# Summing a matrix-vector product over the partitions: products in column strips of the array in place of one-column products

## The chip, the cores and the metric

One core of a Trainium2 chip. The metric is the device time of one execution of the whole kernel in microseconds, the median of several runs; less is better.

## The reference, cut to what matters

A block of DEPTH = 2 layers with adaptive normalisation is followed by a second block that has none. All is fp32, D = 1024, 512 tokens. The part of the change is the first line of each layer of the first block:

```python
cond = jax.nn.silu(c)                                   # (1, 1024)
for i in range(DEPTH):
    mod = (cond @ ada_w[i] + ada_b[i]).reshape(b_, 3, 3, D_MODEL)   # ada_w[i]: (1024, 9216)
    h = adaln(x, norm_g[i, 0], mod[:, 0, 0], mod[:, 0, 1])
    x = x + 0.5 * (1.0 + mod[:, 0, 2][:, None, :]) * swiglu(h, ffn_w_in[i, 0], ffn_w_out[i, 0])
    ...
```

So `mod` holds 9 vectors of 1024 for each layer, 18 in all: shift, scale and gate of three sublayers.

## The kernel before, in words

The activations lie transposed in SBUF, 1024 channels as 8 chunks (DC) of 128 partitions, 512 tokens along the free dimension. Each large product is done in split precision: ScalarE (ACT) rounds a unit of weights (8 x 128 x 128, loaded by SyncE (SP) into one of four stages) to `w_hi` (L778), VectorE (DVE) subtracts to `w_lo` (L1325), and TensorE (PE) does three fp32r products for each chunk (L2060 to L2062; L2075 to L2077 for the first two units behind a norm), 24 matmuls of 512 columns a unit. A step of a feed-forward's first half (`step_in`) is four units, and there are eleven steps (`FC // 2`). `w_hi` and `w_lo` have two sides, so ACT converts a unit when the unit two before it is done.

The conditioning product is not done on PE as a matrix product. `cond` lies as one column for each of the 8 chunks of channels; DVE multiplies a piece of 128 rows and 512 columns of `ada_w` by its scalars and adds it to `ada_acc` (128 x 1024), 16 instructions a vector (`ada_add`, L1338 and L1341). Then `ada_acc` holds, for each of the vector's 1024 elements, 128 parts, one for each partition, and they must be summed over the partitions so that element c * 128 + q lands in partition q, column c. That is `ada_sum` on PE (L2081 to L2088): eight fp32 products, each with a 128 x 128 piece of `ada_acc` as the stationary operand and one column of ones as the moving one, into eight columns of bank 7 (`MODS`). `ada_finish` on DVE (L1344 to L1350) waits for it and adds the bias into `mod`.

The first two vectors (shift and scale of the first norm, `ADA_FIRST = 2`) are made ahead of everything, in `ada_first_acc` (128 x 2048): eight DVE instructions (L2014 to L2022), then `first_modulation` on PE (L2673 to L2679), 16 products behind the statistics of the first norm, while DVE waits at L2025 and adds the bias at L2026. The first norm needs its result: gain (L1358), `sg` (L1391), `h_hi`, `h_lo`, the first products.

The other 16 vectors are made one a step: 7 in the first seven steps of the first feed-forward and 9 in the first nine steps of the second (`ADA_IN = {0: 7, 1: 9}`), all well ahead of their use. The order of work in a step is written out by hand for each engine. DVE does for each of the four units: the conversion of the unit two ahead, for odd ones the product of gate and up (L1443), its share of the 16 additions (`ADA_ADDS = [6, 10, 16, 16, 16]`, the first 6 ahead of the first conversion), `a_lo` (L1450); `ada_finish` comes last in the step. PE does its four units and then `ada_sum`. SP issues the pieces of `ada_w` between the loads of weights, into a ring of eight slots, each freed by the addition that read it (L611); its first load waits for the first modulation (L613). `pe.wait_ge` in `ada_sum` asks that all 16 additions are done and that the vector before was finished; the first addition of a vector waits for the sum of the one before (L1337).

Other places that are compared with: attention's weighing (`weigh`), plain fp32 products with a stationary operand of 64 columns. In L2242 the products of a head follow one another into the same 64 partitions of a bank; in L2604 two heads alternate, one into partitions 0 to 63 and one into 64 to 127, each with widths of 512, 384, 128 and 256. An fp32 product takes two matmul instructions, an fp32r one takes one. DVE at shapes like those of the change: L1548 reduces 128 x 512 from PSUM to one column, L1724 multiplies 128 x 256.

Of the kernel before, what the change touches and what calls it, by code (L numbers as in the profile page):

```python
# [23 lines left out]
ALU = mybir.AluOpType  # L24
ACT = mybir.ActivationFunctionType
AX = mybir.AxisListType

P = 128
S = 512
D = 1024  # L30
DC = D // P
# [10 lines left out]
ADA_FIRST = 2  # L42
# [5 lines left out]
def vec_columns():  # L48

    col, at = {}, 0  # L50
    for name, n in [("c", 8), ("ada_b", 144), ("norm_g", 48), ("pool_scale", 8), ("ln_mix", 16), ("ln_ffn", 16),
# [7 lines left out]

VEC, NVEC = vec_columns()  # L60
CONST = {"ident": 0, "ones": P, "blk64": 2 * P, "blk32": 3 * P, "rot32": 4 * P, "rot96": 5 * P, "mask": 6 * P,
         "dft": 7 * P}
NCONST = 9 * P


class Tally:
# [27 lines left out]
def build(nc, A, out):  # L94
    ctx = ExitStack()
    with ctx:
        def sem(name):
            return ctx.enter_context(nc.semaphore(name))
# [40 lines left out]
        ada_acc = at("ada_acc", [P, D], F32, "ada", 4 * ADA_COLS * 4)  # L139
        ada_first_acc = at("ada_first_acc", [P, ADA_FIRST * D], F32, "ada")  # L140
# [7 lines left out]
        def small(name, n, dt=F32):  # L148
            t = at(name, [P, n], dt, "small", small_at[0])
            small_at[0] += (n * {BF16: 2, U8: 1}.get(dt, 4) + 31) // 32 * 32  # L150
            assert off["small"] + small_at[0] <= SLAB, name
            return t

        vec = small("vec", NVEC)
        consts = small("consts", NCONST)
        ident, ones, blk64, blk32, rot32, rot96, mask = (
            consts[:, CONST[c]:CONST[c] + P] for c in ("ident", "ones", "blk64", "blk32", "rot32", "rot96", "mask"))
        dft = consts[:, CONST["dft"]:CONST["dft"] + 2 * P]
        negident_r = small("negident_r", 16, F32R)
        ident_bf = small("ident_bf", P, BF16)  # L160
        mask_bf = small("mask_bf", P, BF16)
# [8 lines left out]
        mod = small("mod", 18 * DC)  # L170
# [3 lines left out]
        zero = small("zero", DC)  # L174
        eps = small("eps", 1)
        gs = small("gs", S)

        bank = [ctx.enter_context(nc.psum_tensor(f"bank{i}", [P, S], F32)) for i in range(8)]
        GATE, UP, Y, MODS = bank[0:2], bank[2:4], bank[4:6], bank[7]
# [32 lines left out]
        ada_first_added = sem("ada_first_added")  # L212
        mod_summed = sem("mod_summed")
        mod_ready = sem("mod_ready")
        dve_chain = sem("dve_chain")
        x_in_t = sem("x_in_t")
        out_t = sem("out_t")
# [1090 lines left out]
        def _(dve):  # L1308
            n = Tally()
# [18 lines left out]
            def ada_add(m, v=0):  # L1328
# [10 lines left out]
                else:  # L1339
                    dve.wait_ge(ada_added, v * ADA_PER_VEC + u - 1)  # L1340
                    nc.vector.scalar_tensor_tensor(acc, w, cond[:, k:k + 1], acc, ALU.mult, ALU.add) \  # L1341
                        .then_inc(ada_added, 1)

            def ada_finish(v=0):  # L1344
                dve.wait_ge(mod_summed, n.vec - ADA_FIRST + v + 2)
                col = (n.vec + v) * DC
                dst = mod[:, col:col + DC] if isinstance(v, int) else mod[:, bass.ds(col, DC)]
                b = vec[:, VEC["ada_b"] + col:VEC["ada_b"] + col + DC] if isinstance(v, int) else \
                    vec[:, bass.ds(col + VEC["ada_b"], DC)]
                nc.vector.tensor_tensor(dst, MODS[:, 0:DC], b, ALU.add).then_inc(mod_ready, 1)  # L1350

            def norm(s):

# [660 lines left out]
            for k in range(DC):  # L2014
                dve.wait_ge(ada_first_loaded[k], 16)
                if k == 0:
                    ins = nc.vector.tensor_scalar(ada_first_acc[:], ada_first[:, k], cond[:, k:k + 1], None, ALU.mult)
                else:
# [4 lines left out]
            convert(0)  # L2023
            convert(1)
            dve.wait_ge(mod_summed, 1)  # L2025
            nc.vector.tensor_tensor(mod[:, 0:ADA_FIRST * DC], MODS[:, 0:ADA_FIRST * DC],  # L2026
                                    vec[:, VEC["ada_b"]:VEC["ada_b"] + ADA_FIRST * DC], ALU.add) \
                .then_inc(mod_ready, ADA_FIRST)
            n.vec = ADA_FIRST
# [19 lines left out]
        def _(pe):  # L2049
            n = Tally()  # L2050
# [15 lines left out]
            def first_pair(dsts, cols=(P, P)):  # L2066
# [3 lines left out]
                for k in range(DC):  # L2070
                    pe.wait_ge(h_ready, (n.norm - 1) * DC + k + 1)
                    for a, dst in enumerate(dsts):
# [5 lines left out]
                        if k == DC - 1:  # L2078
                            ins.then_inc(unit_done, 1)

            def ada_sum(v=0):  # L2081

                pe.wait_ge(ada_added, (n.vec - ADA_FIRST + v + 1) * ADA_PER_VEC)
                pe.wait_ge(mod_ready, n.vec + v)
                for c in range(DC):
                    ins = nc.tensor.matmul(MODS[:, c:c + 1], ada_acc[:, c * P:(c + 1) * P], ones[:, 0:1],  # L2086
                                           start=True, stop=True)
                ins.then_inc(mod_summed, 1)  # L2088

            def busy_work(spare, count):  # L2090

# [581 lines left out]
            def first_modulation():  # L2673

                pe.wait_ge(ada_first_added, DC)
                for c in range(ADA_FIRST * DC):
                    ins = nc.tensor.matmul(MODS[:, c:c + 1], ada_first_acc[:, c * P:(c + 1) * P], ones[:, 0:1],
                                           start=True, stop=True)
                ins.then_inc(mod_summed, 1)  # L2679

            n.vec = ADA_FIRST
            for step in STAGE_ORDER:
# [14 lines left out]
            for t in range(TB):  # L2697
                for g in range(2):
                    if 2 * t + g >= 4:
                        pe.wait_ge(out_copied, 2 * t + g - 3)  # L2700
                    for d in range(4):
                        c = 4 * g + d
# [67 lines left out]
def constants():  # L2770

    c = np.zeros((P, NCONST), np.float32)
    i = np.arange(P)

    def put(name, a):
        c[:a.shape[0], CONST[name]:CONST[name] + a.shape[1]] = a
    put("ident", np.eye(P))
    put("ones", np.ones((P, P)))
    put("blk64", i[:, None] // 64 == i[None] // 64)
    put("blk32", i[:, None] // 32 == i[None] // 32)  # L2780

    first = (i % 32) < 16
    rot = -1.0 * ((i[:, None] == i[None] + 16) & first[None]) + ((i[:, None] == i[None] - 16) & ~first[None])
    put("rot32", rot)
    rot96 = rot.copy()
    rot96[:64] = rot96[:, :64] = rot96[96:] = rot96[:, 96:] = 0
    put("rot96", rot96)
    put("mask", np.where(i[:, None] >= i[None], 0.0, -1e30))

    f = 2 * np.pi * (i[:, None] * i[None] % 64) / 64  # L2790
    scale = (i[:, None] // 64 == i[None] // 64) / np.sqrt(64.0 * S)
    put("dft", np.concatenate([np.cos(f) * scale, np.sin(f) * scale], 1))
    t = np.arange(S)
    g = 2 * np.pi * (t[:, None] * t[None] % S) / S
    seq = np.stack([np.cos(g), -np.sin(g)]).astype(np.float32)
    bands = []
    for w in (2, 4, 8, 16):
        reach = (i[None] - i[:, None] >= 0) & (i[None] - i[:, None] < w)
        bands += [reach / w - np.eye(P), reach / np.minimum(i + 1, w)[None] - np.eye(P),
                  ((P + i[None] - i[:, None] < w) / w)[:, 0:16]]  # L2800

    inv = (1.0 / (np.float32(10000.0) ** (np.arange(0, 32, 2, dtype=np.float32) / np.float32(32)))).astype(np.float32)
    ang = inv[:, None] * t.astype(np.float32)[None]
    cos, sin = np.tile(np.cos(ang), (2, 1)), np.tile(np.sin(ang), (2, 1))
    rope_m = np.stack([np.concatenate([np.ones((64, S)), cos]), np.concatenate([np.zeros((64, S)), sin])])
    rope_d = np.stack([np.tile(cos, (4, 1)), np.tile(sin, (4, 1))])

    masks = [(i[:, None] // (2 * h) == i[None] // (2 * h)) & (i[:, None] // h != i[None] // h)
             for h in (64, 32, 16, 8, 4, 2, 1)] + [i[:, None] == i[None]]
    return {"consts": c, "dft_seq": seq, "pool_band": np.concatenate(bands, 1).astype(np.float32), "rope_m": rope_m.astype(np.float32),  # L2810
            "rope_d": rope_d.astype(np.float32), "hgrn_mask": np.concatenate(masks, 1).astype(np.float32)}
# [21 lines left out]
```

## Time and profile before

| what | value |
|---|---|
| median of 3 runs | 3809.81 us (3807.85 to 3809.84) |
| span of the profiled execution, first to last instruction | 3808.2 us |
| time of that execution by itself | not among the three listed |
| busy: PE, PE loads of weights, DVE, ACT, POOL | 98%, 77%, 46%, 36%, 3% |
| mean granted TensorE clock | 0.990 |
| DMA | 390 MB, mean 103 GB/s |

Times in the profile are counted from the first instruction. Engines are named PE (TensorE's matmuls), PEld (its loads of weights, which overlap them), DVE, ACT, POOL (GpSimd) and SP. L with a number is a line of the kernel. A matmul's duration in the profile is modelled and longer than the distance to the next one, so the price of a run of matmuls is read from starts.

### The profile page before, as it was taken

Reading aid. Unit: us, or ns where it says so; the run is one execution under the profiler, and the core shown is the slowest. Engines: PE = TensorE matmul, PEld = TensorE weight load, DVE = VectorE, ACT = ScalarE, POOL = GpSimd, SP = SyncE. Lnnn points to the kernel's source line nnn. Section 1 sums busy time; section 2 is a strip of 40 time slices with the busy share of each in tenths; the row PEclk is TensorE's granted clock in tenths of the full one; section 3 lists DMA queues with packets and bytes.
Section 4 is the critical chain, followed back from the end, with each engine's and each line's share of the span. In section 5 each row is a group of like instructions: output and inputs, shape, how many; then the busy total and the mean of one; then the engine's idle time right before and its main releaser. Section 6 shows DMA issues by size and latency. Waiting matters only on the chain.

```text
span 3808.2 us, 45331 instructions
## 1 busy us (share of the span) xinstructions
PE 3714.1 (98%) x16764; PEld 2915.5 (77%) x16764; DVE 1767.0 (46%) x2474; ACT 1371.6 (36%) x2163; POOL 97.3 (3%) x74
## 2 busy tenths in 40 slices
PE   6999999999999999999999999999999999999999
PEld 4888778887888777888767677878876667787887
DVE  6743377424333654433344656443333465644333
ACT  3222432223223554322343435332234444433221
POOL 2000100000000000000000000000000000000000
PEclk8999999999999999999999999999999999999999
DMA  7843268533333212333412222333341222233332
GB/s 267 263 144 96 87 213 268 152 101 89 99 93 96 61 51 72 88 94 94 125 44 67 54 71 56 96 90 95 94 128 47 61 60 64 62 93 89 95 96 85
DMA packets 639949, 390.39 MB, mean 103 GB/s; under 512 B 17856, under 2 KB 601408, under 8 KB 638784
## 3 DMA queue, kind: packets, MB, share of 16 engines
q1 hardware_dynamic: 638080, 383.51, 34.4%
q10 hardware_dynamic: 1728, 4.96, 0.4%
q8 instruction: 93, 1.52, 0.2%
q14 instruction: 48, 0.39, 0.0%
HBM read 386.31 MB, written 2.10 MB: 102 GB/s over the span
## 4 chain that ended last, share of the span: by engine, by line
PE 91%; DVE 5%; ACT 2%; issue 1%; POOL 1%; DMA 0%; DVEq 0%; ACTq 0%; POOLq 0%
PE bank L2060 25%; PE bank L2062 25%; PE bank L2061 25%; PE bank L2242 2%; PE bank L2075 1%; PE bank L2201 1%; PE bank L2077 1%; PE bank L2076 1%; PE bank L2234 1%; POOL ssum L746 1%; PE bank L2182 1%; PE bank L2086 1%; PE bank L2428 1%; DVE work L1724 1%; PE bank L2184 1%
## 5 line engine op out<-in xcount | busy, mean ns | idle before, releaser
L1325 DVE TENSOR_TENSOR w_lo<-stage,w_hi 128x1024 fp32r<-128x1024 f32 x564 | 692.4, 1228 | 1410.8 <-ACT w_hi L778 1410.1
L2060 PE MATMUL bank<-h_hi,w_hi 128*128 128x512 f32 x3064 | 1217.1, 397 | 8.4 <-DVE w_lo L1325 4.7
L2062 PE MATMUL bank<-h_hi,w_lo 128*128 128x512 f32 x3064 | 1195.1, 390 | 0.0
L2061 PE MATMUL bank<-h_lo,w_hi 128*128 128x512 f32 x3064 | 1194.4, 390 | 0.0
L778 ACT ACTIVATE w_hi<-stage 128x1024 fp32r<-128x1024 f32 x564 | 596.8, 1058 | 1223.8 <-PE bank L2062 1211.7
L2060 PEld LDWEIGHTS bank<-h_hi,w_hi 128*128 128x128 f32 x3064 | 576.5, 188 | 144.7 <-issue 18.8
L2061 PEld LDWEIGHTS bank<-h_lo,w_hi 128*128 128x128 f32 x3064 | 576.8, 188 | 123.2 <-issue 6.7
L2062 PEld LDWEIGHTS bank<-h_hi,w_lo 128*128 128x128 f32 x3064 | 575.9, 188 | 121.9
L2062 PE MATMUL bank<-a_hi,w_lo 128*128 128x512 f32 x1056 | 410.8, 389 | 0.0
L2060 PE MATMUL bank<-a_hi,w_hi 128*128 128x512 f32 x1056 | 410.8, 389 | 0.0
L2061 PE MATMUL bank<-a_lo,w_hi 128*128 128x512 f32 x1056 | 410.8, 389 | 0.0
L2061 PEld LDWEIGHTS bank<-a_lo,w_hi 128*128 128x128 f32 x1056 | 198.2, 188 | 41.3
L2062 PEld LDWEIGHTS bank<-a_hi,w_lo 128*128 128x128 f32 x1056 | 198.2, 188 | 41.1
L2060 PEld LDWEIGHTS bank<-a_hi,w_hi 128*128 128x128 f32 x1056 | 198.2, 188 | 41.1
L839 ACT ACTIVATE a_hi<-prod 128x512 f32 (+1 forms) x132 | 83.5, 632 | 263.4 <-DVE prod L1443 263.4
L1450 DVE TENSOR_TENSOR a_lo<-prod,a_hi 128x512 f32 (+1 forms) x132 | 91.3, 692 | 105.6 <-ACT a_hi L839 105.6
L746 POOL TENSOR_TENSOR ssum<-ssum,sq 128x512 f32<-128x512 f32 x60 | 90.7, 1512 | 489.5 <-ACT sq L798 488.0
L1548 DVE TENSOR_REDUCE nmax<-bank 128x1 f32<-128x512 f32 x96 | 62.0, 684 | 67.5 <-PE bank L2227 67.4
L930 ACT ACTIVATE work<-bank,nmax 128x512 f32<-128x512 f32 x96 | 65.1, 687 | 68.9 <-DVE nmax L1548 68.9
L1443 DVE TENSOR_TENSOR prod<-sg,bank 128x512 f32<-128x512 f32 x132 | 89.7, 680 | 0.0
L1341 DVE SCALAR_TENSOR_TENSOR ada_acc<-work,cond,ada_acc 128x512 f32<-128x512 f32 x128 | 88.9, 745 | 0.0
L884 ACT ACTIVATE gs<-bank 128x512 f32<-128x512 f32 x64 | 38.1, 595 | 137.9 <-PE bank L2062 137.3
(291 smaller groups left out, 3343.6 us busy)
## 6 DMA issues: line engine op xcount, KB each, us to landing
stage<-in_ffn_w_in SPq DMA_DIRECT2D x176, 512.0 KB, 3.9
stage<-in_w_in SPq DMA_DIRECT2D x108, 512.0 KB, 4.0
stage<-in_w_gate_up SPq DMA_DIRECT2D x88, 512.0 KB, 3.8
ada_stage<-in_ada_w SPq DMA_DIRECT2D x128, 256.0 KB, 4.1
work<-in_ada_w SPq DMA_DIRECT2D x128, 256.0 KB, 5.5
stage<-in_ffn_w_out SPq DMA_DIRECT2D x64, 512.0 KB, 4.0
stage<-in_w_down SPq DMA_DIRECT2D x32, 512.0 KB, 4.0
stage<-in_ffn_w_out SPq DMA_DIRECT2D x32, 384.0 KB, 3.4
```

The source lines that it names most:

```text
L746: nc.gpsimd.tensor_tensor(ssum[:], ssum[:], chunk(sq, d % 2), ALU.add).then_inc(ss_added, 1)
L778: nc.scalar.activation(weights(u, per * i)[0], stage[:, slot * WORDS:(slot + 1) * WORDS], ACT.Copy).then_inc(w_hi_ready, 1)
L839: nc.scalar.activation(chunk(a_hi, 2 * j + c // 2), chunk(prod, p % 2), ACT.Copy) \
L930: nc.scalar.activation(at_["p"](h, a)[:, b * S:(b + 1) * S], SCORES[(n.block + e) % 3][:], ACT.Exp, bias=nmax[:, col:col + 1], accum_out=r ...
L1325: nc.vector.tensor_tensor(lo, stage[:, slot * WORDS:(slot + 1) * WORDS], hi.bitcast(F32), ALU.subtract).then_inc(w_lo_ready, 1)
L1341: nc.vector.scalar_tensor_tensor(acc, w, cond[:, k:k + 1], acc, ALU.mult, ALU.add) \
L1443: nc.vector.tensor_tensor(chunk(prod, p % 2), chunk(sg, p % 2), UP[p % 2][:], ALU.mult) \
L1450: nc.vector.tensor_tensor(chunk(a_lo, 2 * j + c // 2), chunk(prod, p % 2), chunk(a_hi, 2 * j + c // 2).bitcast(F32), ALU.subtract).then_in ...
L2060: nc.tensor.matmul(dst, wh, chunk(hi, k), start=first and a == 0, stop=False)
L2061: nc.tensor.matmul(dst, wh, chunk(lo, k), start=False, stop=False)
L2062: ins = nc.tensor.matmul(dst, wl, chunk(hi, k), start=False, stop=last and a == len(ks) - 1)
L2242: ins = nc.tensor.matmul(bank[3][rows:rows + 64, :], heads[h]["v"][kc], at_["pt"](kc), start=kc == 0, stop=kc == TB - 1)
```

## The change

Both sums over the partitions (`ada_sum` and `first_modulation`) go through a new `column_sums`. It does four fp32 products: the stationary operand is 32 columns of ones, the moving one is the 32 columns 32j to 32j + 31 of every 128-column piece of the accumulator (8 x 32 = 256 columns for a vector, 16 x 32 = 512 for the first two), and the output goes to partitions 32j to 32j + 31 of bank 7. Every partition p of strip j then holds the sums of all 32 elements q of its strip. DVE picks its own (q = p): it multiplies by a mask of 32 columns, `eye32`, broadcast over the pieces, into `mod_own` (which is the buffer `gs`), waits, reduces 32 columns to one for each piece, waits, and adds the bias as before. The mask grows the constants from 1152 to 1184 columns.

```diff
@@ constants
-         "dft": 7 * P}
-NCONST = 9 * P
+         "dft": 7 * P, "eye32": 9 * P}
+NCONST = 9 * P + 32
@@ vector
+            def own_sums(count, done):
+
+                sums = MODS[:, 0:count * 32].rearrange("p (c i) -> p c i", i=32)
+                own = mod_own[:, 0:count * 32].rearrange("p (c i) -> p c i", i=32)
+                nc.vector.tensor_tensor(own, sums, eye32.to_broadcast([P, count, 32]), ALU.mult) \
+                    .then_inc(mod_masked, 1)
+                dve.wait_ge(mod_masked, done)
+                nc.vector.tensor_reduce(mod_own[:, 0:count], own, AX.X, ALU.add).then_inc(mod_picked, 1)
+                dve.wait_ge(mod_picked, done)
+
             def ada_finish(v=0):
                 dve.wait_ge(mod_summed, n.vec - ADA_FIRST + v + 2)
+                own_sums(DC, n.vec - ADA_FIRST + v + 2)
...
-                nc.vector.tensor_tensor(dst, MODS[:, 0:DC], b, ALU.add).then_inc(mod_ready, 1)
+                nc.vector.tensor_tensor(dst, mod_own[:, 0:DC], b, ALU.add).then_inc(mod_ready, 1)
...
             dve.wait_ge(mod_summed, 1)
-            nc.vector.tensor_tensor(mod[:, 0:ADA_FIRST * DC], MODS[:, 0:ADA_FIRST * DC],
+            own_sums(ADA_FIRST * DC, 1)
+            nc.vector.tensor_tensor(mod[:, 0:ADA_FIRST * DC], mod_own[:, 0:ADA_FIRST * DC],
                                     vec[:, VEC["ada_b"]:VEC["ada_b"] + ADA_FIRST * DC], ALU.add) \
@@ tensor
+            def column_sums(acc, count):
+
+                for j in range(4):
+                    rows = slice(32 * j, 32 * j + 32)
+                    part = acc.rearrange("p (c q) -> p c q", q=P)[:, :, rows]
+                    ins = nc.tensor.matmul(MODS[rows, 0:count * 32], ones[:, 0:32], part, start=True, stop=True)
+                ins.then_inc(mod_summed, 1)
+
             def ada_sum(v=0):
...
-                for c in range(DC):
-                    ins = nc.tensor.matmul(MODS[:, c:c + 1], ada_acc[:, c * P:(c + 1) * P], ones[:, 0:1],
-                                           start=True, stop=True)
-                ins.then_inc(mod_summed, 1)
+                column_sums(ada_acc, DC)
...
                 pe.wait_ge(ada_first_added, DC)
-                for c in range(ADA_FIRST * DC):
-                    ins = nc.tensor.matmul(MODS[:, c:c + 1], ada_first_acc[:, c * P:(c + 1) * P], ones[:, 0:1],
-                                           start=True, stop=True)
-                ins.then_inc(mod_summed, 1)
+                column_sums(ada_first_acc, ADA_FIRST * DC)
```

## Rows read from the trace of the kernel before

**Rows 1.** Page of the profile: busy time by engine, and the last chain by engine

```profile
PE 3714.1 (98%) x16764; PEld 2915.5 (77%) x16764; DVE 1767.0 (46%) x2474; ACT 1371.6 (36%) x2163; POOL 97.3 (3%) x74
...
PE 91%; DVE 5%; ACT 2%; issue 1%; POOL 1%; DMA 0%; DVEq 0%; ACTq 0%; POOLq 0%
```

**Rows 2.** Groups by line: count | busy us, mean ns | idle before, releaser

```profile
L2086 PEld LDWEIGHTS bank<-consts,ada_acc 128*128 128x128 f32 x256 | 31.0, 192 | 3.7 <-DVE ada_acc L1341 2.6
```

**Rows 3.** Timeline of PE, a steady step of the first feed-forward (start us, us)

```profile
102.89 0.39 PE L2062 MATMUL bank<-h_hi,w_lo 128*128 128x512 f32 x1
103.12 1.84 PE L2086 MATMUL bank<-consts,ada_acc 128*128 128x1 f32 x16
...
105.15 0.40 PE L2061 MATMUL bank<-h_lo,w_hi 128*128 128x512 f32 x1
...
126.50 0.39 PE L2062 MATMUL bank<-h_hi,w_lo 128*128 128x512 f32 x1
```

**Rows 4.** Timeline of PE and its loads, weighing of two heads in L2604

```profile
1297.08 2.37 PE L2604 MATMUL bank<-extra,work 128*64 128x512 f32 x16
1299.38 1.13 PE L2541 MATMUL bank<-sq,consts 128*128 128x512 f32 x2
...
1297.56 0.14 PEld L2604 LDWEIGHTS bank<-extra,work 128*64 128x64 f32 x2 [0.29 <-issue]
1297.99 0.14 PEld L2604 LDWEIGHTS bank<-extra,work 128*64 128x64 f32 x2 [0.29 <-issue]
```

**Rows 5.** Timeline of PE, weighing in one half of the partitions in L2242

```profile
2026.16 0.39 PE L2227 MATMUL bank<-work_r 96*128 96x512 f32 x1
2026.48 1.07 PE L2242 MATMUL bank<-extra,work 128*64 128x512 f32 x2
...
2029.65 1.93 PE L2242 MATMUL bank<-extra,work 128*64 128x512 f32 x4
2031.52 0.50 PE L2182 MATMUL bank<-o_parts,wb_hi 128*128 128x512 f32 x1
2031.86 0.40 PE L2183 MATMUL bank<-o_parts,wb_hi 128*128 128x512 f32 x1
```

**Rows 6.** Timeline of PE around the first sum in the first feed-forward

```profile
77.82 2.06 PE L2086 MATMUL bank<-consts,ada_acc 128*128 128x1 f32 x16 [0.91 <-DVE ada_acc L1341]
79.75 0.77 PE L2060 MATMUL bank<-h_hi,w_hi 128*128 128x512 f32 x1
...
83.13 0.39 PE L2062 MATMUL bank<-h_hi,w_lo 128*128 128x512 f32 x1
```

**Rows 7.** Busy time in stretches: PE, PEld, DVE, ACT, POOL, clock, DMA share, GB/s

```profile
50.30:55.60 5.30, 5.30 (x13) 4.19 (x14) 5.20 (x8) 2.45 (x4) 0.00 (x0) 0.50 0.88 301
79.70:82.90 3.20, 3.20 (x9) 2.52 (x10) 2.50 (x7) 0.63 (x1) 0.00 (x0) 0.50 1.07 368
103.00:127.00 24.00, 24.00 (x118) 20.16 (x116) 17.53 (x25) 6.55 (x9) 0.00 (x0) 1.00 0.84 267
```

**Rows 8.** Timeline of PE and DVE, the first modulation

```profile
43.66 3.63 PE L2677 MATMUL bank<-consts,ada_first_acc 128*128 128x1 f32 x32
...
47.40 0.17 DVE L2026 TENSOR_TENSOR mod<-bank,vec 128x16 f32<-128x16 f32 x1 [6.45 <-PE bank L2677]
...
47.61 0.17 DVE L1358 SCALAR_TENSOR_TENSOR gain<-mod,vec 128x8 f32<-128x8 f32 x1
```

**Rows 9.** Groups by line: DVE at the nearest shapes

```profile
L1548 DVE TENSOR_REDUCE nmax<-bank 128x1 f32<-128x512 f32 x96 | 62.0, 684 | 67.5 <-PE bank L2227 67.4
...
L1724 DVE TENSOR_TENSOR work<-work 128x256 f32<-128x256 f32 x128 | 47.4, 433 | 7.9 <-PE bank L2386 7.5
```

**Rows 10.** Timeline of DVE in the same steady step

```profile
111.70 1.23 DVE L1325 TENSOR_TENSOR w_lo<-stage,w_hi 128x1024 fp32r<-128x1024 f32 x1 [0.20 <-ACT w_hi L778]
...
117.14 1.23 DVE L1325 TENSOR_TENSOR w_lo<-stage,w_hi 128x1024 fp32r<-128x1024 f32 x1 [1.56 <-ACT w_hi L778]
```

**Rows 11.** DMA issues from 103 to 180: KB each, median us to landing

```profile
work<-in_ada_w SPq DMA_DIRECT2D x24, 256.0 KB, 5.5
```

More of the change, by code:

```diff
@@ L158, in build @@
         dft = consts[:, CONST["dft"]:CONST["dft"] + 2 * P]
+        eye32 = consts[:, CONST["eye32"]:CONST["eye32"] + 32].rearrange("p (o i) -> p o i", o=1)
         negident_r = small("negident_r", 16, F32R)
@@ L176, in build @@
         gs = small("gs", S)
+        mod_own = gs
         bank = [ctx.enter_context(nc.psum_tensor(f"bank{i}", [P, S], F32)) for i in range(8)]
@@ L214, in build @@
         mod_ready = sem("mod_ready")
+        mod_masked = sem("mod_masked")
+        mod_picked = sem("mod_picked")
         dve_chain = sem("dve_chain")
@@ L2788, in constants @@
     put("mask", np.where(i[:, None] >= i[None], 0.0, -1e30))
+    put("eye32", i[:, None] % 32 == i[None, :32])
     f = 2 * np.pi * (i[:, None] * i[None] % 64) / 64
```

## The prediction

> **What bounds the kernel now.** I read the page first: TensorE (PE) is busy 98% of the span and is 91% of the chain that ended last [rows 1]. So time on PE is time of the kernel wherever PE doesn't wait, and the question is what one conditioning sum costs PE. The groups by line give 256 loads of weights in L2086, each with a matmul of one column (128 products, two instructions each in fp32), and 3.7 us of idle before them in all [rows 2]. Busy time isn't the price, since matmuls and loads overlap. The price is read from the timeline of a steady step of the first feed-forward. From the second matmul after a sum (105.15) to the last before the next (126.50) are 94 pitches: 0.227 us each. From the last matmul ahead of the sum (102.89) to the second behind it (105.15) are 2.26 us where two pitches, 0.45, would do: **a sum costs 1.81 us** [rows 3]. Check: 96 x 0.227 + 1.81 = 23.60, and the step took 126.50 - 102.89 = 23.61. The 16 pairs of load and matmul take 1.84 us of it, some 0.11 each, for one column: the loads of 128 columns of weights set that. 16 such sums are 29 us, 0.76% of the time.
>
> **Per sum, what is removed and added on PE.** Removed: 1.81 us. Added: four products, eight instructions (two passes each), stationary 128x32, moving 256 columns. The price of a pass: in attention's weighing of two heads (L2604) second passes of 512 columns start 0.43 us apart [rows 4], so 0.84 ns a column; 256 columns take 0.215. Do strips run beside one another? L2604 writes two heads alternately to partitions 0-63 and 64-127, in widths 512, 384, 128 and 256, twice each, two passes: 5120 columns of passes, 4.30 us one after another, 2.15 if the two halves run together. It took 2.30 to the next product [rows 4]. L2242, which stays in one half, takes 1.87 us for its four passes of 512, that is 4 x 0.43 + 0.15 [rows 5]. So 0.15 is an exit, and 2.15 + 0.15 = 2.30: **the halves ran together**. Four strips of 32 aren't in this trace. Bounds: all four together, 2 x 0.215 = 0.43; one after another, 1.72. I take 0.43, by the nearest row, which shows no loss at two. Around it: entry 2026.48 - 2026.16 - 0.23 = 0.09 [rows 5], exit 0.15, the first matmul behind it 2031.86 - 2031.52 - 0.23 = 0.11 late [rows 5], and 0.05 for the strips' loads (1297.56 - 1297.08 - 0.43) [rows 4]. New sum: 0.43 + 0.09 + 0.15 + 0.11 + 0.05 = 0.83. Saved 1.81 - 0.83 = 0.98, times 16: **15.7 us**. These edges could be 0.2 more or 0.1 less with four strips: 12.5 to 17.3.
>
> What hides the eight new loads is that PE loads weights while matmuls are in flight. It does so for full arrays: it keeps 0.227 us a matmul of 512 columns [rows 3] although a load of 128 columns takes 0.19 [rows 2]. The Trainium skill (TensorE: Matmul & The Clock Gate, Part 3) says that a load overlaps matmuls in flight only when its row group differs, which here it never does. By that rule, with the page's 1/1.2 ns a column, eight loads of 32 columns would stand bare, an estimated 0.21 us a sum, and the gain would be 12.4 us. The trace disagrees with the rule on full-array products, so I don't take it.
>
> **The first sum pays for the clock too.** At 77.82 PE had waited 0.91 us for VectorE's (DVE's) last addition [rows 6]. After the sum the granted clock is 0.50 (1.2 of 2.4 GHz) until 82.9 [rows 7], and the nine matmuls from 79.75 to 83.13 take 3.38 us, not 2.04 [rows 6]; less the 0.11 that every sum has there, 1.2 are lost. The sum itself was 0.2 slower too (2.06 against 1.84 [rows 3, 6]). The 15 other sums follow dense matmuls and keep 1.00, as 103 to 127 shows [rows 7]. With 0.8 us of 256-column passes in place of 1.9 of single columns I expect the clock not to fall there: gain **1.4**, bound from below by 0 (it falls anyway). The wait stays: DVE's queue decides it.
>
> **First modulation.** 32 instructions run from 43.66, and DVE starts on the result at 47.40: 3.74 us with everything waiting [rows 8]. New: four strips of 512 columns, 2 x 0.43 + 0.09 + 0.05 + 0.15, and 0.11 from PE's end to DVE (47.40 - 47.29) are 1.26. DVE then multiplies by the mask and reduces at 128x512, 0.68 each by the nearest row [rows 9], and each chained step adds 0.04 (47.61 - 47.40 - 0.17 [rows 8]): 1.44 more on the path. Net **1.0 saved**. Bounds: 0.5 lost (mask or reduction at 1.2 us a piece with a broadcast or a strided view, and the clock low) to 2 saved, if the first products, at half clock from 50.3 to 55.6 [rows 7], get it back sooner.
>
> **The same steps per sum on DVE.** Each sum adds a masking multiplication and a reduction at 128x256, 0.43 each by the row nearest in shape [rows 9], and 0.08 for their waits: 0.94 us, 15 in all, ahead of the bias addition; as bounds, 0.8 (overlapped) and 1.5. Nobody waits for the modulation itself then. What is queued behind it is: six additions of the next vector, then the weight conversion w_lo at 111.70 [rows 10]. It waited 0.20 for ACT there, so it would end at 112.93 + 0.94 - 0.20 = 113.7. PE wants it for its third unit, at 102.89 + 0.23 + 1.81 + 2 x 5.45 = 115.8 now, and 1.0 earlier then, 114.8: **1.1 us of slack left**, so it costs nothing. The 1.56 us that DVE idles before 117.14 [rows 10] take up most of the delay in the same step. If that slack went, each us would be a us on PE, sixteen times. The additions also release SP's loads of ada_w, issued up to 0.9 us later: they take 5.5 us to land [rows 11], eight additions ahead of their use, and the weight loads behind them in SP's queue are four units ahead; I take both as covered and keep the doubt as a rival (c). POOL's queue is untouched. Two register waits per loop turn are two of 0.09 us in DVE's sequencer, covered likewise. Constants grow by 16 KB beside 576 KB, ahead of everything, under the wait for x: nothing. The buffer gs isn't used in these stages: nothing.
>
> **Sum:** 15.7 + 1.4 + 1.0 = **18.1 us**. The profiled span is 3808.2; the median of the runs is 3809.8, 1.6 above, which I take as what lies around a span. 3808.2 - 18.1 + 1.6 = **3791.7**.
>
> **Rivals.** (a) *Two strips at a time.* Only two streams of moving data are shown together; each sum then costs 1.26, saves 0.55: 8.8 + 1.4 + 0.2 = 10.4, that is 3799.4. For it: nothing shows four. Against it: no loss at two. (b) *Strips one after another* (the other side): eight passes in a row are 1.72 us, a sum 2.12, 0.31 worse than now; 5.0 on 16, and 2.6 more on the first modulation, whose net becomes a loss of 1.5; with the clock falling as before, 3809.8 + 6.5 = 3816.3. The point that decides is 1.41 us for the four strips of a sum, where 1.81 is reached. Against it: the 2.30 us of L2604. (c) *The step doesn't shrink* because DVE's 0.94 us, or the ring of ada_w loads behind it, becomes the bound: the DMA engines are 84% busy in a steady step [rows 7], and 6.3 MB (267 GB/s in 23.6 us) in 22.6 us instead of 23.6 need 88%. Then the 15.7 stay out and 3809.8 - 2.4 = 3807.4 is left. For it: the loads run only eight additions ahead. Against it: DVE is busy only 17.5 of 24 us [rows 7], and the chain there is PE's.
>
> **How the numbers follow.** Forecast 0.80, (a) 0.07, (b) 0.05, (c) 0.08. The forecast's own range is 12.5 + 0 - 0.5 = 12.0 to 17.3 + 1.4 + 2 = 20.7: 3789.1 to 3797.8. I widen it to 3787 to 3800, which takes in (a) and leaves (b) and (c) out. 0.2%, 7.6 us, is about what a measurement of this kernel can tell from none: the forecast and nearly all of (a) are faster by more, 0.84; (c), (b) as priced and the rest of (a) lie within it, 0.13; slower by over 7.6 would need (b) with DVE late too, 0.03.
>
> **What would show it.** Right: eight matmuls per sum, whose last follows the first by about one pass, and 1.28 us from the last product ahead to the second behind (now 2.26); steps of 22.6 us instead of 23.61; clock 1.00 after the first sum; the first product of the first feed-forward 1 us earlier; DVE's idle time before w_lo smaller, PE's idle unchanged. Wrong: steps of 23.1 (a) or 23.9 (b); or short sums with PE idle on w_lo behind them, or DVE waiting for DMA into ada_stage (c). A clock below 1.00 after the first sum takes 1.4 off.

## The result, and the profile after

| | before | after |
|---|---|---|
| median of 4 runs each | 3809.8 us (3807.9 to 3811.1) | 3784.6 us (3784.3 to 3785.5) |
| ratio, 95% interval | | 0.994 (0.9928 to 0.9952) |
| span of the profiled execution | 3808.2 us | 3782.9 us |

The change is faster, by 25.2 us or 0.7% between these medians (18 to 27 us by the interval). The forecast was 18.1 us and 3791.7, so the sign and the mechanism of the sums held, the gain was put too small, and 3784.6 lies below the stated range of 3787 to 3800. The page of the profile after, to be read against [rows 1]:

```profile
span 3782.9 us, 45061 instructions
...
PE 3686.5 (97%) x16612; PEld 2878.6 (76%) x16612; DVE 1781.0 (47%) x2508; ACT 1371.5 (36%) x2163; POOL 97.4 (3%) x74
...
PEclk8999999999999999999999999999999999999999
...
PE 91%; DVE 5%; ACT 2%; issue 1%; POOL 1%; DMA 0%; ACTq 0%; DVEq 0%; POOLq 0%
```

PE is still 91% of the chain: nothing else became the bound. Now PE in a steady step, the lines that answer to [rows 3] (start us, us):

```profile
98.20 0.39 PE L2078 MATMUL bank<-h_hi,w_lo 128*128 128x512 f32 x1
98.52 0.64 PE L2102 MATMUL bank<-ada_acc,consts 128*32 128x256 f32 x8
99.09 0.50 PE L2076 MATMUL bank<-h_hi,w_hi 128*128 128x512 f32 x1
99.43 0.39 PE L2077 MATMUL bank<-h_lo,w_hi 128*128 128x512 f32 x1
...
120.76 0.39 PE L2078 MATMUL bank<-h_hi,w_lo 128*128 128x512 f32 x1
```

From the last product ahead (98.20) to the second behind (99.43) are 1.23 us instead of 2.26. The step is 120.76 - 98.20 = 22.56 instead of 23.61: **a sum saves 1.05 us**. Eight passes of 256 columns took 0.57 us from the first to the next product, exit included. DVE in the same step, which answers to [rows 10]:

```profile
103.08 0.42 DVE L1352 TENSOR_TENSOR gs<-bank,consts 128x256 f32<-128x256 f32 x1
103.53 0.42 DVE L1355 TENSOR_REDUCE gs<-gs 128x8 f32<-128x256 f32 x1
104.15 0.17 DVE L1365 TENSOR_TENSOR mod<-gs,vec 128x8 f32 x1 [0.20 <-DVE gs L1355]
104.69 0.88 DVE L1342 TENSOR_SCALAR ada_acc<-ada_stage,cond 128x512 f32<-128x512 f32 x2 [0.37 <-issue]
...
108.13 1.22 DVE L1329 TENSOR_TENSOR w_lo<-stage,w_hi 128x1024 fp32r<-128x1024 f32 x1
...
111.91 1.23 DVE L1329 TENSOR_TENSOR w_lo<-stage,w_hi 128x1024 fp32r<-128x1024 f32 x1
```

Mask and reduction take 0.42 each, and the next additions begin at 104.69, 1.6 us after the mask. w_lo ends at 109.35, with none of the 0.20 us idle before it that was there; PE wants it at 98.20 + 0.23 + 0.77 + 10.9 = 110.1. So the slack is 0.75 us where 1.1 was forecast, and the cost is nothing. By the w_lo of 111.91 DVE has not caught up (it used to idle 1.56 us there), but PE wants that one only at 115.6. The first modulation, which answers to [rows 8]:

```profile
43.99 1.06 PE L2102 MATMUL bank<-ada_first_acc,consts 128*32 128x512 f32 x8
...
45.13 0.69 DVE L1352 TENSOR_TENSOR gs<-bank,consts 128x512 f32<-128x512 f32 x1 [4.03 <-PE bank L2102]
45.85 0.69 DVE L1355 TENSOR_REDUCE gs<-gs 128x16 f32<-128x512 f32 x1
46.64 0.18 DVE L2042 TENSOR_TENSOR mod<-gs,vec 128x16 f32<-128x16 f32 x1
...
46.85 0.17 DVE L1373 SCALAR_TENSOR_TENSOR gain<-mod,vec 128x8 f32<-128x8 f32 x1
```

From PE's start to DVE's 1.14 us (before 3.74), then 1.72 to the gain (before 0.21): 2.86 instead of 3.95. And the clock, which answers to [rows 7] (stretch, PE, PEld, DVE, ACT, POOL busy, clock, DMA share, GB/s):

```profile
48.90:52.30 3.40, 2.76 (x7) 2.22 (x8) 3.32 (x6) 1.82 (x3) 0.00 (x0) 0.53 0.92 284
75.00:85.00 10.00, 9.09 (x46) 7.20 (x46) 8.74 (x15) 3.23 (x4) 0.00 (x0) 1.00 1.05 339
98.00:122.00 24.00, 24.00 (x117) 18.75 (x116) 18.20 (x27) 7.29 (x9) 0.00 (x0) 1.00 0.83 263
418.00:438.00 20.00, 17.53 (x112) 14.12 (x111) 9.10 (x15) 12.19 (x23) 0.00 (x0) 1.00 0.42 134
```

No fall behind the first sum (75 to 85), as forecast. But the last line is one that the forecast has no word for. It is the pool mixer, and in the profile of before the same stage, 11 to 12 us later, had the clock down:

```profile
430.00:450.00 20.00, 17.52 (x76) 14.67 (x75) 8.45 (x15) 11.37 (x21) 0.00 (x0) 0.70 0.39 128
```

The distances between the norms' statistics, read from the timelines, say where all of it came from:

| stretch (PE's starts) | before | after | saved |
|---|---|---|---|
| first norm's statistics to the first sum | 41.14 | 39.14 | 2.0 |
| first sum to the second | 25.30 | 22.56 | 2.7 |
| second sum to the second norm's statistics | 326.60 | 320.23 | 6.4 |
| second norm to the third (pool mixer) | 50.08 | 43.85 | **6.2** |
| third norm to the fourth (nine sums) | 386.33 | 376.71 | 9.6 |
| fourth norm to the ninth | 1974.61 | 1974.72 | -0.1 |
| ninth to the last norm | 592.00 | 593.46 | -1.5 |

The sums explain 16 x 1.05 = 16.8 and the clock at the first sum 1.7. Of the 2.0 ahead of the first sum the first modulation has 0.9 (from the statistics to the first product 12.72 instead of 13.61), and 1.1 came with the first products, which got the full clock back at 52.5 instead of 55.6 (the forecast's bound of 2 had allowed for that). 6.2 fell to the pool mixer, in which the change edits nothing, and 1.5 went the other way ahead of the last norm, where the clock was down for 10.2 us instead of 6.8.

### The profile page after: what moved, and what is told of

The parts are those of the page before. It is cut to its first block, busy times and chain, and to the rows that moved or that the text cites. A ratio compares the mean times of both kernels' runs of the same rounds, so it can differ in the third digit from the quotient of the medians.

```text
span 3782.9 us, 45061 instructions
## 1 busy us (share of the span) xinstructions
PE 3686.5 (97%) x16612; PEld 2878.6 (76%) x16612; DVE 1781.0 (47%) x2508; ACT 1371.5 (36%) x2163; POOL 97.4 (3%) x74
## 3 DMA queue, kind: packets, MB, share of 16 engines
HBM read 386.33 MB, written 2.10 MB: 103 GB/s over the span
## 4 chain that ended last, share of the span: by engine, by line
PE 91%; DVE 5%; ACT 2%; issue 1%; POOL 1%; DMA 0%; ACTq 0%; DVEq 0%; POOLq 0%
PE bank L2076 25%; PE bank L2077 25%; PE bank L2078 25%; PE bank L2263 2%; PE bank L2091 1%; PE bank L2222 1%; PE bank L2093 1%; PE bank L2092 1%; PE bank L2255 1%; PE bank L2203 1%; POOL ssum L750 1%; PE bank L2449 1%; PE bank L2407 1%; PE bank L2204 1%; PE bank L2205 1%
## 5 line engine op out<-in xcount | busy, mean ns | idle before, releaser
L2076 PEld LDWEIGHTS bank<-h_hi,w_hi 128*128 128x128 f32 x3064 | 576.0, 188 | 151.2 <-issue 25.3
```

Of the source, the lines that this page charges most:

```text
L2076: nc.tensor.matmul(dst, wh, chunk(hi, k), start=first and a == 0, stop=False)
```

## The experiments

Ratios are to the kernel before, run beside it on the same chip. In experiments 1 and 2 each kernel, the one before included, was executed once, so their times can carry no small difference; what counts there is read from the trace. "Sum to sum" is the distance between PE's starts.

**1. Do the strips run together, and what if not.** All four products of each of the 16 later sums go to one strip; the first modulation stays as changed. It leaves 16 of the 18 modulation vectors without three quarters of their sums.

```diff
-            def column_sums(acc, count):
+            def column_sums(acc, count, one=False):
...
-                    ins = nc.tensor.matmul(MODS[rows, 0:count * 32], ones[:, 0:32], part, start=True, stop=True)
+                    ins = nc.tensor.matmul(MODS[0:32] [:, 0:count * 32] if one else MODS[rows, 0:count * 32], ones[:, 0:32], part, start=True, stop=True)
...
-                column_sums(ada_acc, DC)
+                column_sums(ada_acc, DC, True)
```

> The changed kernel, but the four products of each of the 16 later sums all go to the same column strip, partitions 0 to 31 (the last one stays; the other strips keep old values, so 16 of the vectors of mod are wrong). If the four strips ran together in the change, this costs six more passes of 256 columns, 6 x 0.213 = 1.28 us a sum: steps of 22.56 + 1.28 = 23.84 us, 16 x 1.28 = 20.5 us in all, 3805 and up to 6 more or less by the clock. If they ran two at a time, it costs only four more passes, 0.85: steps of 23.4 us, 3798.

3812.6 us (before 3811.4). Timeline of PE, a steady step:

```profile
100.92 0.39 PE L2078 MATMUL bank<-h_hi,w_lo 128*128 128x512 f32 x1
101.24 1.91 PE L2102 MATMUL bank<-ada_acc,consts 128*32 128x256 f32 x8
103.08 0.50 PE L2076 MATMUL bank<-h_hi,w_hi 128*128 128x512 f32 x1
```

The sum takes 103.08 - 101.24 = 1.84 us instead of 0.57: 1.27 more, six passes of 0.213. In the change a sum costs 22.56 - 96 x 0.227 = 0.77 us of a step. Steps are 23.83 here, so such a sum costs 0.77 + 1.27 = 2.04. In the change, then, **all four strips ran together**, with no loss against two, and without that it would have cost more than the 1.81 us it replaces, as rival (b) said. (The time is 7.7 us more than 3784.6 + 16 x 1.27: the clock was down in the pool mixer here too, with 49.9 us from the second norm to the third instead of 43.9.)

**2. Is the pool mixer's gain a matter of time?** Dense products between the halves of the first feed-forward put everything behind them later, by 2.6, 6.0 and 11.1 us (3, 7 and 13 products).

```diff
...
+  if i == 0:
+      pe.wait_ge(mod_ready, ADA_FIRST + count)
+      busy_work(MODS, 3)
```

> The changed kernel with 3 fp32 products of 128x512 (0.86 us each, 2.6 us of dense work) between the two halves of the first feed-forward, behind the seventh sum; everything from there on comes 2.6 us later. Theory P (whether the clock falls around the pool mixer depends on when the kernel's idle stretches come, so the 6.2 us that the changed kernel won between the second and third norm beyond its shorter sums is luck of the shift): some shifts bring a stretch at 0.50 back into the pool mixer; this one is 2.6 of the 11.0 us by which the pool mixer moved; time 3784.6 + 2.6 = 3787.2, or up to 6.2 more if the clock falls. Theory L (the clock stayed up for a reason that the change brought with it, whatever the time): 3787.2 and no stretch at 0.50 between 415 and 455.

> The same with 7 products, 6.0 us. Theory P: as before, 3790.6 or up to 6.2 more; at least one of the shifts of 2.6, 6.0 and 11.1 us brings the stretch at 0.50 back. Theory L: 3790.6, clock 1.00 in the pool mixer.

> The same with 13 products, 11.1 us: the second norm's statistics start at 418.8 + 11.1 = 429.9, within 0.2 us of where they were before the change. Theory P, time counted from the kernel's start: the stretch at 0.50 is back in the pool mixer (before the change 438 to 451.6), second to third norm 50 us again instead of 43.9: 3784.6 + 11.1 + 6.2 = 3801.9. Theory L: 3795.7 and second to third norm 43.9.

3795.5, 3791.2 and 3794.3 us, where the delay alone gives 3787.2, 3790.6 and 3795.7. Busy time in stretches around the pool mixer, with 2.6 us and with 11.1 us:

```profile
422.00:442.00 20.00, 17.83 (x78) 14.97 (x77) 7.84 (x13) 10.47 (x20) 0.00 (x0) 0.71 0.42 134
```

```profile
430.00:450.00 20.00, 17.43 (x114) 14.15 (x113) 9.62 (x16) 13.02 (x25) 0.00 (x0) 1.00 0.40 129
```

2.6 us later the clock fell (second to third norm 49.75 us), 6.0 and 11.1 us later it didn't (43.8, 44.0). (The first of these also lost 1.7 us to a fall at 65, a step ahead of the first sum, so its mixer came 4.1 us later and not 2.6.) Theory L falls, since the changed kernel can lose the clock there. Theory P as I put it falls as well: with 11.1 us the mixer lay at the times of before and kept the clock. What is left is a guess, that an idle stretch of 2 us ahead of the mixer (PE waits for the pool band) brings the clock down in some executions and not in others.

**3. Filling that idle stretch**, in both kernels.

```diff
-  busy_work(bank[3], 3)
+  busy_work(bank[3], 5 if n.norm == 1 else 3)
```

> The kernel before the change, with five in place of three products of ones by constants (0.86 us each) behind the statistics of the norm ahead of the pool mixer, where PE idled for 2.0 us until the pool band landed. They take no time of their own. Theory P (the clock's fall in the pool mixer, 6.2 us, hangs on how that idle stretch lies in time, and the changed kernel only happened to miss it): the clock stays at 1.00 from 415 to 465, second to third norm 43.9 us instead of 50.1, time 3809.8 - 6.2 = 3803.6. Theory L (the fall has nothing to do with that idle stretch): 3809.8.

> The same edit to the changed kernel, where the clock didn't fall there: unchanged, 3784.6. With the run of the filled kernel before, the difference is what the change does with the pool mixer's clock taken out: 3803.6 - 3784.6 = 19.0 by theory P (25 by theory L).

3807.2 (10 runs) against 3807.0 for the kernel before (13 runs), ratio 0.9999 (0.9989 to 1.0008); and 3784.3, ratio 0.9934 (0.9918 to 0.9951). The filled kernel before:

```profile
80.00:84.00 4.00, 4.00 (x10) 3.10 (x10) 4.00 (x8) 0.00 (x0) 0.00 (x0) 0.50 1.10 347
430.00:450.00 20.00, 19.37 (x118) 15.02 (x117) 9.10 (x16) 12.51 (x24) 0.00 (x0) 1.00 0.40 134
```

The mixer was at 1.00 and took 43.7 us, 6.4 less than in the first profile, yet the time is the same: a miss for theory P's 3803.6. In this execution the clock was down longer behind the first sum (sum to sum 26.88 us, not 25.30) and at other places later. That pointed to the next experiment, which also shows why this one can't prove what the filling does: the mixer keeps the clock in some executions without it. Over all sixteen profiles the clock fell in the mixer in five of the ten executions without filling there and in none of the six with it, which speaks for the filling and doesn't settle it.

**4. The same two kernels, profiled once more.**

> The kernel before, unchanged, another execution profiled. Theory P2 (the moments at which the clock can change lie differently in each execution, so which idle stretches bring it down is drawn anew each time): the stretches at 0.50 after 45 us differ from the first profile's, in the pool mixer perhaps none; the steps with a sum are 23.61 us again. Theory P (they are fixed in the kernel's time): the same stretches again, 438 to 451.6 among them. Both: PE at 0.50 behind the first sum, near 79, for 3.4 or 6.8 us, 1.7 or 3.3 us lost.

> The changed kernel, unchanged, another execution profiled. Steps with a sum 22.56 us, the first step 22.56 too, with no stretch at 0.50 near 76 to 85. Theory P2: the stretches at 0.50 elsewhere differ from the first profile's, the pool mixer may have one. The time against the kernel before on this chip: 16 x 1.05 + 0.9 + 1.7 to 3.3 = 19.4 to 21.0 us less, plus or minus what the clock does elsewhere, some 3.

3807.8 against 3807.5 (ratio 1.0001), and 3785.4 against the same 3807.5, ratio 0.9942 (0.9929 to 0.9956), 22.1 us. The kernel before, unchanged:

```profile
80.00:84.00 4.00, 4.00 (x11) 3.13 (x10) 3.56 (x8) 0.00 (x0) 0.00 (x0) 0.50 1.11 345
430.00:450.00 20.00, 17.66 (x115) 14.34 (x115) 9.62 (x16) 13.02 (x25) 0.00 (x0) 1.00 0.40 132
```

The changed kernel, unchanged:

```profile
80.00:84.00 4.00, 4.00 (x19) 3.30 (x19) 3.81 (x8) 1.54 (x2) 0.00 (x0) 1.00 1.02 302
426.00:430.00 4.00, 4.00 (x25) 3.77 (x24) 1.68 (x2) 2.75 (x5) 0.00 (x0) 0.63 0.00 0
```

**The observation that P2 makes is shown**: identical instructions, but in the first profile of before the clock was down from about 438 to 452 and in this one not at all there; instead it stayed down twice as long behind the first sum (6.8 us, not 3.4; 26.88 us sum to sum). The changed kernel had a short fall in the mixer at 426 this time and none there in its first profile. The reason that P2 gives for it (when the clock can change) no run shows. The spans of these two are 3803.2 and 3782.3, 20.9 apart instead of 25.3, and here the account closes without the mixer's 6.2: 16.8 for the sums, 0.9 for the first modulation, 3.3 behind the first sum, and -0.1 for all the rest.

**5. One half of the change alone**: first only the 16 later sums in strips, then only the first modulation.

> Only the 16 later sums in strips; the first modulation by 16 one-column products and without mask and reduction, as before. The first sum then follows the same PE work as before the change, at the same time. My theory: the clock stays at 1.00 after the first sum (gain 1.7), 16 sums give 16 x 1.05 = 16.8, and the first modulation's own 0.9 is missing: 3784.6 + 0.9 = 3785.5, or 6.2 more if the clock falls in the pool mixer. Rival: the clock at the first sum was the first modulation's doing, by its earlier end: then it falls to 0.50 after the first sum, and 1.7 more are missing.

> Only the first modulation by strips, mask and reduction; the 16 later sums by one-column products. It is worth 0.9 us alone, plus 0 to 1.1 if the first products get the full clock sooner, within what a comparison can tell: 3806 to 3808 on this chip. The first sum: if the one-column products behind a wait are what brings the clock down, 0.50 shows near 78 to 85 as before the change; if the earlier first modulation keeps it up, it doesn't.

Only the sums: 3786.7 against 3807.0, ratio 0.9945 (0.9928 to 0.9961), 2.4 us short of the filled changed kernel timed beside it, where 0.9 was expected; the two intervals overlap. Only the first modulation: 3807.2 against 3807.5, ratio 0.9998: its 1 us is below what can be measured (the ten executions took 3804.3 to 3814.2 us, and the profiled one was the slowest). The clock behind the first sum, sums only:

```profile
76.00:80.00 4.00, 3.31 (x20) 2.44 (x21) 2.84 (x4) 1.69 (x2) 0.00 (x0) 1.00 1.08 359
80.00:84.00 4.00, 4.00 (x20) 3.30 (x19) 3.77 (x9) 0.97 (x1) 0.00 (x0) 1.00 1.09 337
```

Only the first modulation, with sums of one-column products:

```profile
80.00:84.00 4.00, 4.00 (x20) 3.30 (x19) 3.36 (x6) 0.10 (x1) 0.00 (x0) 1.00 1.11 346
430.00:450.00 20.00, 17.73 (x77) 15.27 (x76) 7.88 (x12) 9.30 (x16) 0.00 (x0) 0.66 0.32 107
510.00:518.00 8.00, 8.00 (x27) 6.61 (x27) 5.91 (x10) 0.63 (x1) 0.00 (x0) 0.57 1.08 354
```

The strips keep the clock although the first modulation is the old one, so the rival for the first sum falls. With one-column sums it stayed up at the first sum this once but fell at the first sum of the *second* feed-forward (510 to 518, sum to sum 26.88), the other one that follows a wait of about 0.9 us for DVE. Over the four executions with old sums and no filling ahead of them (first profile, before_pool_filled, before_again, first_only) behind the sums in these two places 1.7, 3.3, 3.3 and 3.3 us were lost; in all eleven executions with sums of 256 moving columns, none. The wait isn't always there: in 11 of the 32 places the clock had already fallen about 12 us ahead of the sum, with old sums and new ones alike, and PE came so late that nothing was left to wait for. Counted by sums behind a wait, the clock fell in four of seven with one-column products and in none of thirteen with strips.

**6. Keeping the clock up by dense products in PE's idle time**, 14 or 21 of them ahead of the first norm.

```diff
   def norm():
       n.xchunk += DC
+      busy_work(bank[7] if n.norm == 0 else bank[3], {0: 21, 2: 6}.get(n.norm, 0))
       pe.wait_ge(ss_added, (DC - 1) * (n.norm + 1))
...
-      busy_work(bank[3], 3)
+      busy_work(bank[3], 3 + (2 if n.norm == 1 else 0))
...
       column_sums(ada_first_acc, ADA_FIRST * DC)
+      busy_work(bank[3], 4)
```

> The changed kernel with such products wherever PE idles around the first three norms: 14 ahead of the first norm's statistics (into bank 7, while PE idles 19 us), 4 behind the first modulation, 2 more ahead of the pool mixer, 6 ahead of the third norm's statistics. If PE has the full clock there: the first norm's statistics and the three products behind them take 3.4 us less PE time, of which about 2.5 are on the path to the first modulation; the first products at full clock gain up to 1.1, the products behind the third norm 1.7 to 3.4 (half of 3.4 to 6.8 us at 0.50). 3784.6 - 6 = 3778 to 3779. If the clock doesn't rise by such products, they only delay: 3785 to 3790.

> As kept_warm, but 21 products ahead of the first norm's statistics in place of 14, so that they end at 36.1, 0.7 us before the statistics can start (with 14 they ended at 30.1 and the clock fell at 32.8). If dense products hold the clock: 1.00 from the statistics to the first products, the first modulation done 2.5 us earlier, the first products up to 1.1 more: 3 to 4 us below the changed kernel. If the clock falls all the same: no gain, and 0.3 lost where the products end too late.

The diff is that with 21. With 14: 3783.9, ratio 0.9935, no gain over the 3784.3 beside it. PE had nothing to do from 30.1 to 36.8, the clock fell at 32.8, and the statistics ran at 1.2 GHz:

```profile
31.00:37.00 6.00, 0.18 (x1) 0.18 (x2) 5.79 (x3) 3.92 (x5) 5.62 (x2) 0.65 1.18 291
37.00:43.00 6.00, 6.00 (x12) 3.73 (x13) 4.19 (x3) 1.71 (x4) 0.00 (x0) 0.50 0.21 51
```

With 21 products, PE's timeline and two stretches:

```profile
18.02 18.19 PE L2114 MATMUL bank<-consts 128*128 128x512 f32 x42
36.57 1.13 PE L2123 MATMUL bank<-ssum,consts 128*128 128x256 f32 x4 [0.36 <-POOL ssum L750]
...
41.07 1.06 PE L2102 MATMUL bank<-ada_first_acc,consts 128*32 128x512 f32 x8
...
46.61 0.47 PE L2091 MATMUL bank<-h_hi,w_hi 128*128 128x512 f32 x1 [0.85 <-DVE h_lo L1392]
```

```profile
37.00:50.00 13.00, 12.15 (x45) 6.36 (x44) 11.42 (x17) 4.75 (x9) 0.00 (x0) 1.00 0.44 131
400.00:460.00 60.00, 55.50 (x295) 43.73 (x294) 31.27 (x41) 32.55 (x51) 11.16 (x8) 1.00 0.28 91
```

The clock is at 1.00 from the statistics on, the first modulation's products start at 41.07 instead of 43.99 and the first product at 46.61 instead of 49.54. 3781.7 us against 3785.4 for the changed kernel and 3807.5 for the one before, ratio to the latter 0.9936 (0.9923 to 0.995). By its median it is the fastest kernel of the study, by 3.7 us, but the intervals of the two ratios overlap.

**7. The same products in the kernel before** (three instead of four behind the first modulation), to compare the two with the clock kept up in both.

> The kernel before the change with the dense products of kept_warm_longer: 21 ahead of the first norm's statistics, 3 behind the first modulation (PE idles only 3.0 us there, 4 would be late), 2 more ahead of the pool mixer, 6 ahead of the third norm's. With the clock up through the first 470 us in both kernels, the difference to kept_warm_longer is the change's own: 16 x 1.05 + 0.9 = 17.7, plus 0 to 3.3 if the one-column products behind a wait still bring the clock down at the first sum of a feed-forward. So if my account (about 20.5 of the 22 to 25 us are the change's, the rest is what the clock happened to do at other places) holds: 3781.7 + 17.7 to 21 = 3799.4 to 3802.7. Rival, all 22 to 25 us are the change's own: 3804 to 3807, no faster than the plain kernel before.

> The same kernel as kept_warm_longer, timed beside before_kept_warm on one chip: 3781.7, 3.0 to 3.7 below the changed kernel.

On one chip: 3800.8 us (11 runs, ratio 0.9981, 0.9972 to 0.999) and 3780.9 us (5 runs, ratio 0.9929, 0.9915 to 0.9943), with 3808.5 for the plain kernel before. The difference is **19.9 us**, inside 17.7 to 21, and the rival as priced (3804 to 3807, no faster than the plain kernel before) is out: the filling alone takes 7.6 us off the kernel before and some 3.7 off the changed one (experiment 6). But the clock wasn't kept up in both. The filled kernel before, in its profiled execution:

```profile
37.00:50.00 13.00, 13.00 (x53) 8.78 (x53) 8.51 (x13) 4.02 (x8) 0.00 (x0) 0.77 0.33 93
...
60.00:76.00 16.00, 14.21 (x56) 11.29 (x55) 13.32 (x18) 6.06 (x7) 0.00 (x0) 0.89 0.80 253
```

The changed kernel had 1.00 from 37 to 50. Here the first modulation's one-column products ran from 41.28, right behind dense products and at full clock, and 2.8 us into them, at 44.1, the clock fell until 51.0. The three filling products behind them then ran at half clock and ended at 49.8, 1.5 us after the first product's operands were there. And there was a second fall from 64.6 to 68.0, which left nothing of the wait ahead of the first sum:

```profile
76.28 1.84 PE L2086 MATMUL bank<-consts,ada_acc 128*128 128x1 f32 x16
...
99.88 1.84 PE L2086 MATMUL bank<-consts,ada_acc 128*128 128x1 f32 x16
```

99.88 - 76.28 = 23.60, so this sum lost nothing. The two profiled spans, 3796.7 and 3779.1, differ by 17.6. That this is the 17.7 of the sums and the first modulation is luck: 3.8 us (not 0.9) lie between the first norm's statistics and the first sum, for the reasons just given, and 3.1 went the other way ahead of the last norm, where the changed kernel had the clock down longer. The 17.7 rests on the steps (23.61 and 22.56) and on the first modulation's path, not on this pair.

## Why the prediction was too small

- **"A sum costs 1.81 us" and what bounds it** held: PE's chain, steps of 23.61 us, the loads of 128 columns.
- **"New sum 0.83, saved 0.98."** Right mechanism (the four strips together), 0.06 too dear: 0.77 was measured. Entry (0.09) and the late second product (0.11) were as read from L2242. The middle was priced 0.63 and is 0.57: the 0.05 that L2604 showed ahead of its second passes don't add here. 16 x 0.07 = **1.1 us** of the error.
- **The rule that was set aside.** By the Trainium skill (TensorE: Matmul & The Clock Gate, Part 3), loads would have stood bare, and the sum would have cost 0.83 + 0.21 = 1.04 us by the forecast's terms. The trace disagrees again: 0.77 was measured. The same section of the Trainium skill also lets a load go ahead into the background weight buffer, and the 0.77 would fit that. (16 x 0.21 off the 15.7 leave 12.3, not 12.4.)
- **"First modulation 1.0 saved."** Held: 3.95 - 2.86 = 1.1 from its own start, 0.9 from the statistics to the first product; mask and reduction at 0.69 each against 0.68.
- **The clock at the first sum, "gain 1.4".** Right that it doesn't fall with strips. Wrong in size twice. The forecast's own rows give 1.7: from the start at 79.75 to the start at 83.13 are eight pitches and not nine, so 1.82 should have been taken off and not 2.04 (sum to sum says the same, 25.30 - 23.61). And the profile of before showed one of its shorter falls: with old sums two places can pay, and four executions lost 1.7 to 3.3 us. This is the term that was most undersized among those that belong to the change.
- **DVE's additions cost nothing**: held, with 0.75 us of slack instead of 1.1, since the chained steps wait longer in the loop (0.20 ahead of the bias addition, 0.37 ahead of the next vector) than outside it, where 0.04 was read. PE's idle time ahead of w_lo didn't grow.
- **The step of the forecast that failed** is the last one, "15.7 + 1.4 + 1.0 = 18.1" and "3808.2 - 18.1 + 1.6". It took the span of one profiled execution for the kernel's time and put the clock everywhere but at the first sum at nothing, as if it were a fixed property of the kernel. The runs show that the falls differ between executions of identical instructions (experiment 4). In the first pair of profiles this gave the change 6.2 us in the pool mixer and 1.1 at the first products, and took 1.5 back late in the kernel: 5.8 of the 7.1 us by which the forecast was short. The other 1.3 are the sums (1.1) and the clock at the first sum (0.3), less 0.1 at the first modulation. On two later occasions the medians differ by 22.7 (the changed kernel with the mixer's gap filled) and 22.1.
- **The range** reached down to 3787 by the bounds of the forecast's own terms (20.7 us, 3789.1) and 2 us more. The spread of the clock belonged in it: the plain kernel before took anything from 3803.8 to 3812.3 us in its executions.
- Rivals (a), (b), (c): out, by the 0.57 us, by experiment 1, and by steps of 22.56.

What stays open: of 22 to 23 us in the plain comparison some 20.6 are accounted for (16.8, 0.9, and on average 2.9 of clock at the sums). The mean granted clock of all timed executions says that the clock's share isn't only chance: it is 0.9905 over 60 executions of the kernel before and 0.9923 over nine of the changed one, and executions of the kernel before at 0.991 took 1.8 us less than those at 0.990, so the difference is worth an estimated 3.3 us, 21.0 in all. Where beside the two first sums the changed kernel keeps the clock, the sixteen profiles don't settle: without filling, the mixer's long fall came in two of three executions with old sums and in two of seven with new ones.

## What to carry to other kernels

A sum over partitions with a one-column moving operand is paid in loads of weights: turning it round, with ones as a 32-column stationary operand and the data streaming through the four column strips at once, costs two fp32 passes of a quarter of the data, provided that a little vector work to pick out the result has slack to hide in. Before forecasting a change of half a per cent from one profile, look for the stretches at half clock: here they came and went between executions, and such stretches belong in the range. Profile each kernel a second time before explaining a difference by them. Dense filler in the idle time, ending less than a microsecond before the work came, kept the clock up around the first norm of the changed kernel; in the kernel before, one-column products brought it down in spite of the filler, which then ended late.

## What the runs showed of the hardware beyond the forecast

- Four fp32 products in four column strips, 128 rows deep, ran at the pace of one: 0.57 us for eight passes of 256 columns, 1.84 us in one strip.
- The granted clock of the same kernel differed from execution to execution in place and length. At 1.2 GHz the pool mixer's opening cost 6.2 us. A PE wait of 0.8 to 0.9 us and then 1.8 us of one-column matmuls brought the clock down in four of seven cases, the same wait and then 0.6 us of strips in none of thirteen, and the same wait and then 1.84 us of 256-column matmuls not in the one case there is (one_strip).
- One-column matmuls brought the clock down without any wait as well: at 44.1 in before_kept_warm, 2.8 us after they took over from dense products at full clock.
- Filler that ended 6.7 us ahead of the work was worth nothing; in the changed kernel filler that ended 0.4 us ahead kept 2.4 GHz from the first norm until 478 us, in both executions profiled.
